# Keys and values projected between the two query chunks, the first attention two slots sooner

## The chip, the cores and the metric

The kernel runs on one core of one Trainium2 chip. The metric is the device time of one execution in microseconds (us), as the median of several runs; lower is better.

## The reference, cut to what matters

Two transformer-like blocks are computed for 256 tokens of width 1024. The first block projects the normed input into z, xbc, dt, q, k, v and gates, runs a state-space branch (a depthwise convolution of xbc, SiLU, a scan in two directions) and a window attention, mixes both with gates, and ends with an MLP. The second block has its own attention, a short convolution and an MLP. The change touches only the attention of the first block and the order in which its inputs are projected:

```python
proj = h @ w_in[l]
z, xbc, dt_raw, q, k, v, gates = split_cols(proj, IN_SPLITS)
...
logits = jnp.einsum('bnqgrd,bnkgd->bngrqk', qb, kb).astype(jnp.float32) * (ATTN_HEAD_DIM ** -0.5)
...
logits = jnp.where(valid[None, :, None, None], logits + bias, -jnp.inf)
m = jnp.maximum(jnp.max(logits, axis=-1, keepdims=True), sink_l)
p = jnp.exp(logits - m)
p = p / (jnp.sum(p, axis=-1, keepdims=True) + jnp.exp(sink_l - m))
out = jnp.einsum('bngrqk,bnkgd->bnqgrd', p.astype(v.dtype), vb)
```

There are 16 query heads and 4 key/value heads of 64. With 256 tokens there are two query blocks (token halves) of 128.

## The kernel before, in words

**Slots.** All weights are streamed from memory as 146 pieces of 1 MB plus the small dt piece, one for each of 147 slots, in an order written out by hand (`STRETCHES`, L119). SyncE issues the loads into a ring of three raw buffers. For each slot ScalarE rounds the piece into `w_hi` (`split_hi`, L1053) and VectorE computes the rest `w_lo` (`split_lo`, L1422), both two slots ahead of TensorE. TensorE multiplies three products (hi by hi, hi by lo, lo by hi) for each part (L393). The first slots are: 0 and 1 first half of the queries, 2 dt, 3 and 4 second half of the queries, 5 and 6 keys and values, 7 and 8 the first chunk of xbc, 9 and 10 of z, 11 to 24 seven more chunks of xbc.

**Work between the slots.** Every engine walks over the slots in the same program order, and side work is written into fixed places of this walk: the middle of a slot on TensorE (`slot_middle`, after half of its products) or its end. An engine takes its instructions in order, so a wait holds up all that is written behind it on that engine.

**The attention of the first block** is cut into eight units a = 0 to 7, each of four heads and one token half. Unit a goes through a pipeline of places:

- slot 7+a, end, TensorE: `scores` (L750), 8 small matmuls into banks 4 and 5.
- slot 7+a, VectorE: `softmax_sink` (L1564 to L1571), adds the bias table `bias1`, takes the maximum. Before it in the same slot stands `split_lo`.
- slot 8+a, ScalarE: `exps` (L1114); VectorE: `softmax_divide` (L1602, L1603), only the reciprocal, placed behind the `softmax_sink` of the next unit; GpSimd: `softmax_times` (L2059), multiplies the probabilities by it.
- slot 9+a, end, TensorE: `prob_turn` (L765), transposes half 0, then (after the scores of unit a+2) half 1 into bank 7; ScalarE: `prob_out` (L1149), copies both out.
- slot 10+a, middle, TensorE: `values1` (L775) into bank 7; ScalarE: `values_hi` (L1134); VectorE: `values_lo` (L1593), which frees bank 7.

The unit numbering takes all four query tiles of token half 0 first, then those of token half 1 (`r = a // 4`, `u = a % 4`).

**Other side work near it.** `softplus` and `minus_log_dt` (L1634 to L1651) compute dt and its negative logarithm on VectorE in small dependent steps; they stand in slots 4 and 6. `decay_sums` (L809) stands in slot 9. The convolution of chunk c: ScalarE copies it out (L1261) and applies the middle tap (L1268), VectorE applies the other four (`conv_taps`, L1663) in two halves of 8 instructions, chunk 0 in slots 9 and 10, chunk 1 in 13 and 14, chunk 2 in 15 and 16. SiLUs stand in slot 15 on ScalarE: the first chunk of z (L1238), then conv chunks 0 and 1 (L1144), which need another activation table than the exponentials; `exps` of unit 7 stands behind them in the same slot. `conv_turn` (L801) transposes finished chunks from slot 16 on.

The diff touches the places above in the programs of TensorE, ScalarE and VectorE, and the order of the pieces. GpSimd's and SyncE's programs keep their text.

Of the kernel before, what the change touches and what calls it, by code (L numbers as in the profile page):

```python
# [70 lines left out]

S_Q = 0
S_DT = 2
S_KV = 5
S_XBC = 7
S_Z0 = 9
S_XBC1 = 11
# [29 lines left out]
for _name, _width in PARAMS:  # L107
# [6 lines left out]
SILU_AT = {15: (0, 1), 19: (2, 3), 21: (4,), 23: (5,), 25: (6,)}  # L114
# [2 lines left out]


STRETCHES = [  # L119
    ("q", S_Q, "feat", 2), ("dt", S_DT, "dt", 1), ("q", S_DT + 1, "feat", 2), ("kv", S_KV, "kv", 2), ("xbc", S_XBC, "feat", 2),  # L120
    ("z", S_Z0, "tok", 2), ("xbc", S_XBC1, "feat", 14), ("z", S_Z, "tok", 6), ("gate", S_GATE, "tok", 8), ("ao", S_AO, "acc", 4), ("so", S_SO, "acc", 8),
    ("wo", S_WO, "acc", 4), ("mi", S_MI, "wide", 16), ("mo", S_MO, "acc", 16),
    ("q2", S_Q2, "tok", 2), ("k2", S_K2, "tok", 2), ("v2", S_V2, "tok", 2), ("cb2", S_CB2, "feat", 2),
# [1 line left out]
    ("ab2", S_AB2, "acc", 2), ("cv2", S_CV2, "acc", 2), ("wo2", S_WO2, "acc", 4),  # L125
    ("mi2", S_MI2, "wide", 16), ("mo2", S_MO2, "acc", 16),
]


def slot_table():  # L130
# [17 lines left out]
def build(nc, w_stream, w_dt, x_in, params_in, table_in, onehot_in, gate_bias_in, post_in, rpb_in,  # L148
# [3 lines left out]
    with ctx:  # L152
# [205 lines left out]
        def emptied(eng, key):  # L358

            eng.wait_ge(drained[where[key][0]], where[key][1] + 1)  # L360
# [12 lines left out]
        def _(pe):  # L373
# [367 lines left out]

            def scores(name, a, q_tile, k_tile):

                r = a // (4 if name == "a1" else 2)
                claim((name + "s", a, 0), 4)
                claim((name + "s", a, 1), 5)
                for h in range(2):
                    for e in range(2):
                        rows = slice(e * HD, e * HD + HD)
                        ins = pe.matmul(ps[:, 4 + e, h * TOK:h * TOK + TOK],  # L750
                                        q_tile(h)[rows, (1 - r) * P:(1 - r) * P + P], k_tile(h)[rows, :],
                                        start=True, stop=True)
                        if h:
                            ins.then_inc(*fill_of((name + "s", a, e)))
# [12 lines left out]
                ins.then_inc(*fill_of(key))  # L767

            def values1(a):
                kv = 2 * (a % 4 // 2)  # L770
                claim(("a1o", a), 7)
                emptied(pe, ("a1p", a, 1))
                for jt in range(RT):
                    for e in range(2):
                        ins = pe.matmul(ps[e * HD:e * HD + HD, 7, 0:2 * P],  # L775
                                        v_tok[:, jt, (kv + e) * HD:(kv + e) * HD + HD],
                                        prob_t1[a % 2][:, jt, 2 * e:2 * e + 2], start=jt == 0, stop=jt == 1)
                ins.then_inc(*fill_of(("a1o", a)))
# [95 lines left out]

            def slot_middle(s):

                if 0 <= s - 10 < 8:
                    values1(s - 10)
                if 0 <= s - 97 < 4:
                    values2(s - 97)  # L880
                if s in TURN_AT:
                    conv_turn(TURN_AT[s])
                if 0 <= s - 28 < GROUPS:
                    ssd_decay(s - 28, 1)
                if 0 <= s - 29 < GROUPS:
                    ssd_states(s - 29)
                    ssd_diagonal(s - 29)
                    ssd_across(s - 29)
# [8 lines left out]
            for s in range(SLOTS):  # L897
# [26 lines left out]
                if s == 0:  # L924
# [4 lines left out]
                    claim("rel", 4)  # L929
                    pe.matmul(ps[0:Q_HEADS, 4, :], table[:, :], onehot[:, :], start=True,  # L930
                              stop=True).then_inc(*fill_of("rel"))
                if s == 9:
                    decay_sums()

                if 0 <= s - 9 < 8:
                    prob_turn("a1", s - 9, 0, logit1)
                if s == S_DT + 1:

                    emptied(pe, "dt")
                    claim("dt_turn", 6)  # L940
                    for r in range(RT):
                        ins = pe.transpose(ps[:, 6, r * 64:r * 64 + 64], dt_feat[0:64, r * P:r * P + P],
                                           ident[0:64, 0:64])
                    ins.then_inc(*fill_of("dt_turn"))
                if 0 <= s - 7 < 8:
                    tile = 4 * ((s - 7) % 4 // 2) + 2 * ((s - 7) % 2)
                    if s == 7:
                        for c in range(2):
                            for h in range(2):
                                emptied(pe, ("q", c, h))  # L950
                        emptied(pe, ("kv", 0, 0)), emptied(pe, ("kv", 0, 1))
                    scores("a1", s - 7, lambda h: q_t[:, tile + h, :], lambda h: k_t[:, tile // 4, :])
                if 0 <= s - 9 < 8:
                    prob_turn("a1", s - 9, 1, logit1)
                if s == 17:
                    cumulate()

# [79 lines left out]
        def _(act):  # L1037
# [91 lines left out]
                                   ACT.Exp).then_inc(*drain_of(key))  # L1129

            def values_hi(a):
                r, tile = a // 4, 2 * (a % 4)
                ready(act, ("a1o", a))
                act.activation(ot_hi[:, tile:tile + 2, r * P:r * P + P],  # L1134
                               ps[:, 7, 0:2 * P].rearrange("p (h i) -> p h i", h=2),
                               ACT.Copy).then_inc(ot_hi_ready, 1)
# [50 lines left out]
            for s in range(SLOTS):  # L1187
# [35 lines left out]
                if s == S_DT + 1:  # L1223
                    act.wait_ge(dt_neg, 1)
                    act.activation(dtw[:, 2], dtw[:, 1], ACT.Exp).then_inc(dt_exp, 1)
                if 0 <= s - 10 < 8:
                    values_hi(s - 10)
                if s in TURN_AT:
                    c = TURN_AT[s]
                    ready(act, ("turn", c, 0))  # L1230
# [7 lines left out]
                    act.activation(zg(all_rows, 0, 512), zg(all_rows, 0, 512), ACT.Silu).then_inc(z_first_silu, 1)  # L1238
                for c in SILU_AT.get(s, ()):
                    conv_active(c)  # L1240
                if s == 9:
                    ready(act, "sums")
                    act.activation(sums[:, :, :], ps[:, 7, 0:4 * HEADS].rearrange("p (a b) -> p a b", a=4),
                                   ACT.Exp).then_inc(*drain_of("sums"))

                if 0 <= s - 8 < 8:
                    exps(s - 8, logit1, 0, True)

                if name == "xbc" and closes:
                    c = chunk  # L1250
# [13 lines left out]
                    for i in range(4):  # L1264
                        if i % 2 == 0:
# [1 line left out]
                        f = 4 * c + i  # L1267
                        act.activation(acc_of(c)[:, i, :], conv_in[k][:, i, PAD:PAD + TOK], ACT.Identity,  # L1268
                                       scale=conv_w[:, 2, f:f + 1], bias=conv_b[:, f:f + 1]).then_inc(conv_tap0, 1)
                if 0 <= s - 9 < 8:  # L1270
                    prob_out("a1", s - 9, 0, prob_t1)
                    prob_out("a1", s - 9, 1, prob_t1)
                if s == 18:
                    ready(act, "cum")
                    act.activation(cum_hi[:, :, :], ps[:, 6, :].rearrange("p (u l) -> p u l", u=4),
# [134 lines left out]
        def _(dve):  # L1410
# [139 lines left out]

            def softmax_sink(a):

                k, r, u = a % 2, a // 4, a % 4
                sink, at0 = param("sink"), P * (1 - r)
                if a == 0:
                    dve.wait_ge(bias1_landed, 16)
                if a >= 2:
                    ready(dve, ("a1p", a - 2, 1))
                for e in range(2):
                    key = ("a1s", a, e)  # L1560
                    ready(dve, key)
                    for h in range(2):
                        i, head = 2 * e + h, 8 * (u // 2) + 2 * (u % 2) + 4 * e + h
                        ins = dve.tensor_tensor_reduce(logit1[k][:, i, :], ps[:, 4 + e, h * TOK:h * TOK + TOK],  # L1564
                                                       bias1[:, head, at0:at0 + TOK], 1.0,
                                                       sink[:, 4 * u + i:4 * u + i + 1], ALU.add, ALU.max,
                                                       soft[:, k, 0, i:i + 1])
                    ins.then_inc(*drain_of(key))
                emptied(dve, ("a1s", a, 0)), emptied(dve, ("a1s", a, 1))
                link(dve.tensor_scalar(soft[:, k, 1, :], soft[:, k, 0, :], -1.0, None, ALU.mult))  # L1570
                dve.tensor_tensor(soft[:, k, 2, :], soft[:, k, 1, :], sink[:, 4 * u:4 * u + 4],  # L1571
                                  ALU.add).then_inc(negmax_ready, 1)
# [15 lines left out]
                dve.tensor_scalar(soft[:, k, 1, :], soft[:, k, 0, :], -1.0, None, ALU.mult).then_inc(negmax_ready, 1)  # L1588

            def values_lo(a):  # L1590
                r, tiles = a // 4, slice(2 * (a % 4), 2 * (a % 4) + 2)
                dve.wait_ge(ot_hi_ready, a + 1)
                dve.tensor_tensor(ot_lo[:, tiles, r * P:r * P + P],  # L1593
                                  ps[:, 7, 0:2 * P].rearrange("p (h i) -> p h i", h=2),
# [200 lines left out]
            for s in range(SLOTS):  # L1795
                if 0 <= s - 28 < GROUPS:
                    ssd_weigh(s - 28, 0)
                if 0 <= s - 10 < 8:
                    values_lo(s - 10)
                if s in TURN_AT:  # L1800
                    c = TURN_AT[s]
                    ready(dve, ("turn", c, 1))
# [25 lines left out]
                                             ALU.min).then_inc(dt_neg, 1)  # L1828
                if s == S_DT + 2:
                    softplus()  # L1830
                if s == S_DT + 4:
                    minus_log_dt()
                if 0 <= s - 7 < 8:
                    softmax_sink(s - 7)
                if 0 <= s - 8 < 8 and s not in SILU_AT:
                    softmax_divide(s - 8, logit1, 0, True)
                if s in TAPS_AT:
                    conv_taps(TAPS_AT[s], (0, 1))
                if s - 1 in TAPS_AT and s != LAST_TAPS:
                    conv_taps(TAPS_AT[s - 1], (2, 3))  # L1840
                if 0 <= s - 8 < 8 and s in SILU_AT:
                    softmax_divide(s - 8, logit1, 0, True)
                if s == 10:
                    emptied(dve, "sums")
                    for i in range(2):
# [278 lines left out]
def packed(inputs):  # L2124
# [17 lines left out]
    w2 = f["w_in_2"][0]  # L2142
    parts = []
    for stretch in (
        pieces_tok(q, 0, 2), pieces_tok(w_in, COL_KV, 1), pieces_tok(w_in, COL_XBC, 1),
        pieces_tok(w_in, COL_Z, 1), pieces_tok(w_in, COL_XBC + 512, 7), pieces_tok(w_in, COL_Z + 512, 3), pieces_tok(w_in, COL_GATE, 4), pieces_acc(ao),
        pieces_acc(f["w_ssd_out"][0]), pieces_acc(f["w_o"][0]), pieces_tok(f["w_mlp_in"][0], 0, 8),
        pieces_acc(f["w_mlp_out"][0]), pieces_tok(w2, 0, 10), pieces_acc(f["w_attn_branch_2"][0]),
# [68 lines left out]
```

## Time and profile before

| what | value |
|---|---|
| median of 3 runs | 947.56 us (947.48 to 947.64) |
| profiled execution, its own time | 949.15 us |
| its span, first to last instruction | 947.3 us |
| TensorE matmul busy | 935.9 us, 99% |
| VectorE busy | 666.1 us, 70% |
| ScalarE busy | 510.2 us, 54% |
| GpSimd busy | 78.8 us, 8% |
| mean granted TensorE clock | 0.998 |

The busy share of TensorE is modelled from pipelined matmuls, so it hides small gaps. The list of waits and the chain of work that ended last show where TensorE waited for another engine. Times in rows are microseconds from the start of the span.

### The profile page before, as it was taken

The numbers are of one execution on the slowest core, as the hardware profiler recorded it, in microseconds if no ns is written. First come the engines' busy times: TensorE is split into PE (matmuls) and PEld (weight loads), VectorE is DVE, ScalarE is ACT, GpSimd is POOL, SyncE is SP. The second block draws the span as 40 slices with busy tenths as digits, with TensorE's granted clock in tenths as the row PEclk, the third lists the DMA queues.
The fourth block names the chain that finished last, engine by engine and source line by source line (L and its number), as shares of the span: only waits on it lengthen the run. The fifth ranks groups of instructions, "written<-read, shape, count | busy, mean of one in ns | idle before, by whom it ended". The sixth has DMA issues, their size and how long they took to land.

```text
span 947.3 us, 13184 instructions
## 1 busy us (share of the span) xinstructions
PE 935.9 (99%) x5362; PEld 808.5 (85%) x5362; DVE 666.1 (70%) x917; ACT 510.2 (54%) x666; POOL 78.8 (8%) x76
## 2 busy tenths in 40 slices
PE   8999989999999999999999999999999999999998
PEld 7988879988888878888888888899888898888887
DVE  6779789998788764778776466767665758776433
ACT  6456886776545733465554335756653455554331
POOL 1002111023321000000002320000000000000000
PEclk9999999999999999999999999999999999999999
DMA  8943233555224385435556955353364435445551
GB/s 306 339 159 122 99 131 112 181 171 177 95 89 156 134 305 185 178 134 212 187 178 212 275 182 219 117 207 131 127 217 181 177 134 220 180 178 221 179 178 45
DMA packets 25276, 166.51 MB, mean 176 GB/s; under 512 B 2986, under 2 KB 3114, under 8 KB 6656
## 3 DMA queue, kind: packets, MB, share of 16 engines
q1 hardware_dynamic: 22464, 156.12, 46.0%
q0 software_dynamic: 2752, 9.54, 3.4%
q8 instruction: 43, 0.70, 0.3%
q14 instruction: 17, 0.14, 0.0%
HBM read 164.57 MB, written 1.08 MB: 175 GB/s over the span
## 4 chain that ended last, share of the span: by engine, by line
PE 90%; DVE 6%; ACT 2%; issue 1%; DMA 0%; DVEq 0%; ACTq 0%
PE ps L393 58%; PE ps L624 11%; PE ps L626 6%; DVE conv_acc L1663 2%; PE ps L821 1%; PE ps L750 1%; PE ps L765 1%; PE ps L424 1%; PE ps L426 1%; PE ps L433 1%; PE ps L512 1%; PE ps L590 1%; DVE logit L1564 1%; PE ps L871 1%; PE ps L801 1%
## 5 line engine op out<-in xcount | busy, mean ns | idle before, releaser
L1422 DVE TENSOR_TENSOR w_lo<-raw,w_hi 128x2048 fp32r<-128x2048 f32 x145 | 336.6, 2327 | 182.2 <-ACT w_hi L1053 182.1
L1053 ACT ACTIVATE w_hi<-raw 128x2048 fp32r<-128x2048 f32 x145 | 275.5, 1905 | 183.7 <-PE ps L393 161.9
L393 PE MATMUL ps<-w_hi,ht 128*128 128x512 f32 (+1 forms) x576 | 181.4, 388 | 0.0
L624 PE MATMUL ps<-ht,w_hi 128*128 128x512 f32 x448 | 158.4, 399 | 0.0
L393 PE MATMUL ps<-ht,w_hi 128*128 128x256 f32 (+1 forms) x816 | 151.3, 287 | 0.0
L393 PEld LDWEIGHTS ps<-ht,w_hi 128*128 128x128 f32 (+1 forms) x816 | 127.1, 192 | 3.3 <-issue 3.3
L393 PEld LDWEIGHTS ps<-w_hi,ht 128*128 128x128 f32 x576 | 107.3, 188 | 22.4 <-issue 1.1
L626 PE MATMUL ps<-ht,w_lo 128*128 128x256 f32 x448 | 125.8, 281 | 0.0
L393 PE MATMUL ps<-ht,w_lo 128*128 128x256 f32 (+1 forms) x408 | 115.7, 283 | 0.0
L393 PE MATMUL ps<-w_lo,ht 128*128 128x512 f32 (+1 forms) x288 | 110.5, 384 | 0.0
L624 PEld LDWEIGHTS ps<-ht,w_hi 128*128 128x128 f32 x448 | 84.2, 188 | 20.8
L393 PE MATMUL ps<-w_hi,ff_hi 128*128 128x512 f32 x256 | 99.7, 389 | 0.0
L393 PE MATMUL ps<-w_hi,ff_lo 128*128 128x512 f32 x256 | 99.6, 389 | 0.0
L393 PE MATMUL ps<-w_lo,ff_hi 128*128 128x512 f32 x256 | 99.6, 389 | 0.0
L626 PEld LDWEIGHTS ps<-ht,w_lo 128*128 128x128 f32 x448 | 84.6, 189 | 0.0
L393 PEld LDWEIGHTS ps<-ht,w_lo 128*128 128x128 f32 (+1 forms) x408 | 78.1, 191 | 0.0
L393 PEld LDWEIGHTS ps<-w_lo,ht 128*128 128x128 f32 x288 | 54.2, 188 | 10.5
L1663 DVE SCALAR_TENSOR_TENSOR conv_acc<-conv_in,params,conv_acc 128x256 f32<-128x256 f32 x128 | 58.9, 532 | 0.0
L393 PEld LDWEIGHTS ps<-w_hi,ff_hi 128*128 128x128 f32 x256 | 48.1, 188 | 10.1
L393 PEld LDWEIGHTS ps<-w_hi,ff_lo 128*128 128x128 f32 x256 | 48.0, 188 | 9.9
L393 PEld LDWEIGHTS ps<-w_lo,ff_hi 128*128 128x128 f32 x256 | 48.1, 188 | 9.9
L1161 ACT ACTIVATE ff_sum<-ps 128x512 f32<-128x512 f32 x32 | 18.8, 595 | 37.6 <-PE ps L626 32.6
(300 smaller groups left out, 1228.5 us busy)
## 6 DMA issues: line engine op xcount, KB each, us to landing
raw<-in_w_stream SPq DMA_DIRECT2D x145, 1024.0 KB, 4.8
bias<-rel_scratch POOLq DMA_DIRECT2D x1, 3072.0 KB, 21.4
bias<-in_rpb POOLq DMA_DIRECT2D x16, 128.0 KB, 8.3
x_first<-in_x_in SPq DMA_DIRECT2D x2, 512.0 KB, 4.1
raw<-in_w_stream SPq DMA_DIRECT2D x2, 512.0 KB, 6.3
gates<-in_gate_bias POOLq DMA_DIRECT2D x4, 256.0 KB, 5.9
gates<-in_gate_bias POOLq DMA_DIRECT2D x2, 512.0 KB, 7.7
x<-in_x_in POOLq DMA_DIRECT2D x1, 1024.0 KB, 8.4
```

Of the source, the lines that this page charges most:

```text
L393: ins = pe.matmul(o, still, moving, start=first and n == 0, stop=last and n == 2, skip_group_check=True)
L424: pe.matmul(ps[:, i, 0:TOK], hi[:, c], ht_hi[:, k, :], start=opens and kt == 0, stop=False, skip_group_check=True)
L426: pe.matmul(ps[:, i, 0:TOK], lo[:, c], ht_hi[:, k, :], start=False, stop=False, skip_group_check=True)
L433: ins = pe.matmul(ps[:, i, TOK:2 * TOK], hi[:, kt * 512 + i * P:kt * 512 + i * P + P], ht_lo[:, 4 * part + kt, :], start=False, stop=close ...
L512: pe.matmul(ps[:, bank0 + r, :], ht_hi[:, 4 * part + kt, tokens], w[:, kt * 512:kt * 512 + 512], start=part == 0 and kt == 0 and m == 0, s ...
L590: pe.matmul(ps[:, 2 * n + r, :], a_hi[:, kt, r * P:r * P + P], w[:, cols], start=kt == 0 and m == 0, stop=False, skip_group_check=True)
L624: pe.matmul(ps[:, b, :], hi[:, c], ht[:, :, k, :], start=opens and kt == 0, stop=False, skip_group_check=True)
L626: ins = pe.matmul(ps[:, b, 0:TOK], lo[:, c], ht_hi[:, k, :], start=False, stop=closes and kt == 3, skip_group_check=True)
L1053: act.activation(split_home(s)[0][:, 0:width(s)], raw[s % RAW_RING][:, 0:width(s)], ACT.Copy).then_inc(hi_ready, 1)
L1161: act.activation(ff_sum[half][:, :, :], ps[:, b:b + 2, TOK:2 * TOK], ACT.Copy).then_inc(lows_out, 1)
L1422: dve.tensor_tensor(lo[:, 0:width(s)], raw[s % RAW_RING][:, 0:width(s)], hi[:, 0:width(s)].bitcast(F32), ALU.subtract).then_inc(lo_ready, 1)
L1663: ins = dve.scalar_tensor_tensor(acc_of(c)[:, i, :], conv_in[k][:, i, tap:tap + TOK], conv_w[:, tap, f:f + 1], acc_of(c)[:, i, :], ALU.mul ...
```

## The change

The second query chunk and the keys and values swap places in the stream: slots 3 and 4 are keys and values, slots 5 and 6 the second query chunk. All places of the attention units move two slots ahead: scores in 5+a, exps and divide in 6+a, the turn in 7+a, values in 8+a. Units take another order: for query tiles 0 and 1 both token halves first (a = 0 to 3), then for tiles 2 and 3 (`unit1`). `decay_sums` with its ScalarE exponential moves from slot 9 to slot 6. `minus_log_dt` moves from slot 6 to slot 11, ahead of that slot's `softmax_sink`. The diff, cut where a line only repeats the shift:

```diff
@@ -71,7 +71,8 @@
 S_Q = 0
 S_DT = 2
-S_KV = 5
+S_KV = 3
+S_Q1 = 5
 S_XBC = 7
@@ -117,7 +118,7 @@
 STRETCHES = [
-    ("q", S_Q, "feat", 2), ("dt", S_DT, "dt", 1), ("q", S_DT + 1, "feat", 2), ("kv", S_KV, "kv", 2), ("xbc", S_XBC, "feat", 2),
+    ("q", S_Q, "feat", 2), ("dt", S_DT, "dt", 1), ("kv", S_KV, "kv", 2), ("q", S_Q1, "feat", 2), ("xbc", S_XBC, "feat", 2),
...
+def unit1(a):
+
+    return a // 2 % 2, 2 * (a // 4) + a % 2
...
             def scores(name, a, q_tile, k_tile):
 
-                r = a // (4 if name == "a1" else 2)
+                r = unit1(a)[0] if name == "a1" else a // 2
...
             def values1(a):
-                kv = 2 * (a % 4 // 2)
+                kv = 2 * (unit1(a)[1] // 2)
...
             def slot_middle(s):
 
-                if 0 <= s - 10 < 8:
-                    values1(s - 10)
+                if 0 <= s - 8 < 8:
+                    values1(s - 8)
...
-                if s == 9:
+                if s == 6:
                     decay_sums()
 
-                if 0 <= s - 9 < 8:
-                    prob_turn("a1", s - 9, 0, logit1)
+                if 0 <= s - 7 < 8:
+                    prob_turn("a1", s - 7, 0, logit1)
...
+                if 0 <= s - 5 < 8:
+                    tile = 2 * unit1(s - 5)[1]
+                    if s == 5:
+                        emptied(pe, ("kv", 0, 0)), emptied(pe, ("kv", 0, 1))
+                    if s in (5, 9):
+                        for h in range(2):
+                            emptied(pe, ("q", (s - 5) // 4, h))
+                    scores("a1", s - 5, lambda h: q_t[:, tile + h, :], lambda h: k_t[:, tile // 4, :])
                 if 0 <= s - 7 < 8:
-                    tile = 4 * ((s - 7) % 4 // 2) + 2 * ((s - 7) % 2)
-                    if s == 7:
-                        for c in range(2):
-                            for h in range(2):
-                                emptied(pe, ("q", c, h))
-                        emptied(pe, ("kv", 0, 0)), emptied(pe, ("kv", 0, 1))
-                    scores("a1", s - 7, lambda h: q_t[:, tile + h, :], lambda h: k_t[:, tile // 4, :])
-                if 0 <= s - 9 < 8:
-                    prob_turn("a1", s - 9, 1, logit1)
+                    prob_turn("a1", s - 7, 1, logit1)
@@ scalar
-                if 0 <= s - 10 < 8:
-                    values_hi(s - 10)
+                if 0 <= s - 8 < 8:
+                    values_hi(s - 8)
...
-                if s == 9:
+                if s == 6:
                     ready(act, "sums")
...
-                if 0 <= s - 8 < 8:
-                    exps(s - 8, logit1, 0, True)
+                if 0 <= s - 6 < 8:
+                    exps(s - 6, logit1, 0, True)
...
-                if 0 <= s - 9 < 8:
-                    prob_out("a1", s - 9, 0, prob_t1)
-                    prob_out("a1", s - 9, 1, prob_t1)
+                if 0 <= s - 7 < 8:
+                    prob_out("a1", s - 7, 0, prob_t1)
+                    prob_out("a1", s - 7, 1, prob_t1)
@@ vector
-                if 0 <= s - 10 < 8:
-                    values_lo(s - 10)
+                if 0 <= s - 8 < 8:
+                    values_lo(s - 8)
...
-                if s == S_DT + 4:
+                if s == 11:
                     minus_log_dt()
-                if 0 <= s - 7 < 8:
-                    softmax_sink(s - 7)
-                if 0 <= s - 8 < 8 and s not in SILU_AT:
-                    softmax_divide(s - 8, logit1, 0, True)
+                if 0 <= s - 5 < 8:
+                    softmax_sink(s - 5)
+                if 0 <= s - 6 < 8 and s not in SILU_AT:
+                    softmax_divide(s - 6, logit1, 0, True)
                 if s in TAPS_AT:
                     conv_taps(TAPS_AT[s], (0, 1))
...
@@ packed, the order of the pieces in memory
-        pieces_tok(q, 0, 2), pieces_tok(w_in, COL_KV, 1), pieces_tok(w_in, COL_XBC, 1),
+        pieces_tok(q, 0, 1), pieces_tok(w_in, COL_KV, 1), pieces_tok(q, 512, 1), pieces_tok(w_in, COL_XBC, 1),
```

## Rows read from the trace of the kernel before

**Rows 1.** The page: busy time of each engine (share of the span), instructions.

```profile
PE 935.9 (99%) x5362; PEld 808.5 (85%) x5362; DVE 666.1 (70%) x917; ACT 510.2 (54%) x666; POOL 78.8 (8%) x76
```

**Rows 2.** Waits of PE, 54 to 150 us: total, times, longest.

```profile
PE ps L775 <- ACT prob_t L1149: 1.8, 1, 1.8
PE ps L765 <- DVE ot_lo L1593: 1.3, 2, 1.0
```

**Rows 3.** Chain that ended last, 54 to 150 us: start, duration, what.

```profile
124.53 1.06 ACT conv_acc L1144
125.61 1.28 ACT L1114
...
131.27 1.74 PE ps L801 x8
133.00 3.73 PE ps L393 x24
...
137.61 2.88 PE ps L393 x24
...
141.53 1.02 PE ps L801 x8
```

**Rows 4.** PE in order of time: start, duration; in brackets the idle time before.

```profile
96.24 0.60 PE L765 MATMUL ps<-params,logit 128*128 128x128 f32 x4
...
124.89 0.66 PE L765 MATMUL ps<-params,logit 128*128 128x128 f32 x4 [0.97 <-DVE ot_lo L1593]
...
130.19 1.08 PE L775 MATMUL ps<-prob_t,v_tok 128*64 128x256 f32 x8 [1.77 <-ACT prob_t L1149]
```

**Rows 5.** Windows; the third number from the end is the granted clock.

```profile
131.00:131.50 0.50, 0.50 (x6) 0.30 (x3) 0.00 (x0) 0.50 (x1) 0.50 (x1) 0.92 0.33 131
...
131.50:134.50 3.00, 3.00 (x16) 3.00 (x15) 1.88 (x3) 1.70 (x4) 0.96 (x1) 0.50 0.01 3
135.00:138.50 3.50, 3.50 (x32) 3.50 (x31) 3.50 (x8) 1.73 (x4) 0.00 (x0) 1.00 0.41 115
```

**Rows 6.** DVE in order of time: first step of minus_log_dt, and what follows its last.

```profile
47.25 0.22 DVE L1638 TENSOR_SCALAR dtw<-dt 128x128 int32<-128x128 int32 x1
...
53.27 2.28 DVE L1422 TENSOR_TENSOR w_lo<-raw,w_hi 128x2048 fp32r<-128x2048 f32 x1
```

**Rows 7.** DVE in order of time, from the end of slot 9 to slot 15.

```profile
71.27 0.48 DVE L1564 CUSTOM_DVE_ANT_0 logit<-ps,bias,params 128x256 f32<-128x256 f32 x1 [2.07 <-PE ps L765]
...
73.66 4.86 DVE L1663 SCALAR_TENSOR_TENSOR conv_acc<-conv_in,params,conv_acc 128x256 f32<-128x256 f32 x8
...
88.67 2.27 DVE L1422 TENSOR_TENSOR w_lo<-raw,w_hi 128x2048 fp32r<-128x2048 f32 x1
90.87 0.47 DVE L1564 CUSTOM_DVE_ANT_0 logit<-ps,bias,params 128x256 f32<-128x256 f32 x1
...
93.14 0.18 DVE L1603 RECIPROCAL soft<-soft 128x4 f32<-128x4 f32 x1
...
126.95 3.25 DVE L1663 SCALAR_TENSOR_TENSOR conv_acc<-conv_in,params,conv_acc 128x256 f32<-128x256 f32 x8
```

**Rows 8.** POOL in order of time: the bias table's load, and one multiplication.

```profile
22.57 1.20 POOL L2035 DMA_DIRECT2D bias<-rel_scratch  x1 [4.56 <-DMA rel_scratch<-rel_row]
...
93.40 1.89 POOL L2059 TENSOR_TENSOR logit<-logit,soft 128x1024 f32<-128x1024 f32 x1 [7.85 <-DVE soft L1603]
```

**Rows 9.** The page's DMA issues: the bias table, us to landing.

```profile
bias<-rel_scratch POOLq DMA_DIRECT2D x1, 3072.0 KB, 21.4
```

**Rows 10.** Chain that ended last, 20 to 56 us: slots 4 to 7.

```profile
31.28 23.23 PE ps L393 x192
54.51 1.06 PE ps L750 x8
```

**Rows 11.** ACT in order of time: the table load of slot 19.

```profile
157.87 1.28 ACT L1144 ACT_TABLE_LOAD   x1
```

**Rows 12.** DVE in order of time, slot 18.

```profile
156.08 0.69 DVE L1726 TENSOR_TENSOR cum_lo<-ps,cum_hi 128x512 f32<-128x512 f32 x1 [1.93 <-ACT cum_hi L1275]
```

More of the change, by code:

```diff
@@ L1131, in values_hi @@
             def values_hi(a):
-                r, tile = a // 4, 2 * (a % 4)
+                r, u = unit1(a)
+                tile = 2 * u
                 ready(act, ("a1o", a))
@@ L1551, in softmax_sink @@
             def softmax_sink(a):
-                k, r, u = a % 2, a // 4, a % 4
+                k, (r, u) = a % 2, unit1(a)
                 sink, at0 = param("sink"), P * (1 - r)
@@ L1590, in values_lo @@
             def values_lo(a):
-                r, tiles = a // 4, slice(2 * (a % 4), 2 * (a % 4) + 2)
+                r, u = unit1(a)
+                tiles = slice(2 * u, 2 * u + 2)
                 dve.wait_ge(ot_hi_ready, a + 1)
@@ L1840, in _ @@
                     conv_taps(TAPS_AT[s - 1], (2, 3))
-                if 0 <= s - 8 < 8 and s in SILU_AT:
-                    softmax_divide(s - 8, logit1, 0, True)
+                if 0 <= s - 6 < 8 and s in SILU_AT:
+                    softmax_divide(s - 6, logit1, 0, True)
                 if s == 10:
```

## The prediction

> **What bounds the kernel now.** I read the page first: TensorE is busy 935.9 us, 99% of the span [rows 1]. The change adds and takes away no matmul, so it can only move waits of TensorE and its clock. The list of waits comes next. In the stretch that the change touches TensorE waits three times: twice for `values_lo` to free bank 7, 1.3 us together, once for `prob_out`, 1.8 us [rows 2]. TensorE in order of time gives each its place: 0.97 us before the second half-turn of slot 15 and 1.77 us before the values in the middle of slot 16 [rows 4]; the third is the rest, 1.3 - 0.97 = 0.3 us, at the end of slot 11. The chain explains the 1.77 us. In slot 15 ScalarE does the SiLUs, the last one ready only after VectorE's taps, then loads the table of the exponentials again for 1.28 us, and only then takes the exponentials of unit 7 and `prob_out` of unit 6, for which TensorE waits [rows 3].
>
> The windows show something behind it. The granted clock is 1.00 until 131, 0.50 from 131.4 to 134.5 at least, and 1.00 again from 135 [rows 5]: 2.4 GHz, 1.2 GHz, 2.4 GHz. Ahead of the fall stand the idle 0.97 and 1.77 us. The eight transposes of slot 16 take 1.74 us there against 1.02 in slot 17, and 24 matmuls 3.73 against 2.88 [rows 3]: (1.74 - 1.02) + (3.73 - 2.88) = 1.6 us. So this jam costs 0.97 + 1.77 + 1.6 = **4.3 us**.
>
> **What the change removes.** Exponentials end in slot 13 and the turns in slot 14, so no exponential stands behind slot 15's SiLUs; one 1.28 us load there and one in slot 19 go with it. Values of unit 7 stand in slot 15, before the SiLUs in ScalarE's order. At the end of slots 15 and 16 no half-turn waits for bank 7 any more. All of the 4.3 us goes. The 0.3 us at slot 11 stays, since taps of chunk 0 remain in slots 9 and 10 ahead of `values_lo`.
>
> **What it moves at no cost.** The matmuls of the stream are the same, 192 in 23.23 us for four slots [rows 10]. Swapping the pieces keeps sizes, count and ring order on SyncE and both splits. The copies of keys and values go to slots 3 and 4 on ScalarE, those of the second query chunk to 5 and 6; each takes the place of the other. The sums in slot 6 are the same instructions, under the exponential table as before. The eight units are the same work in another order. The first scores come after slot 5, at 31.28 + 2 x 5.81 = 42.9, done by 44.0. The bias table is issued at 22.57 and lands 21.4 us later, at 44.0 [rows 8, 9]; if its 1.2 us of issue come on top, 45.2. VectorE then waits 1.2 us, with only the split for slot 8 behind it (2.3 us, needed near 60), and TensorE does not wait. Cover gone would mean a landing after about 50, where the next scores want banks 4 and 5: bounded below by nothing, above by perhaps 1 us. I take 0. The table load removed in slot 19 is hidden: VectorE is synchronised with TensorE through ScalarE's copy in slot 18, for which it idles 1.93 us [rows 11, 12], so behind slot 18 all starts at the same distance from TensorE as before.
>
> **What it adds.** `minus_log_dt` leaves slot 6 for slot 11: 53.27 - 47.25 = **6.0 us** of dependent small steps [rows 6]. In slot 6 VectorE had room. In slot 11 the steps stand between the split for slot 13 and `softmax_sink` of unit 6, and behind that comes the reciprocal of unit 5. GpSimd multiplies only after it, and TensorE turns unit 5 at the end of slot 12. I follow this chain in the times of before, where units 4 and 3 stand in these places. All from the end of slot 9 is the same in both kernels: sink at 71.27, taps from 73.66, and so on with no idle time on VectorE, to the split of slot 11 at 88.67 and the sink at 90.87, the reciprocal at 93.14 [rows 7], GpSimd from 93.40 to 95.29 [rows 8]. TensorE comes to the turn at 96.24 to 96.4 [rows 4]. The slack is about 1 us. With 6.0 us put in ahead of the sink GpSimd ends at 101.3 and TensorE starts at 101.4: **a wait of 5.0 us**. Everything behind it on TensorE is late by that: scores of unit 7 and slot 13.
>
> Behind it I find no second wait. `prob_out` of unit 5 has ScalarE's exponentials of unit 6, a copy of chunk 1 and its four taps ahead of it, and ends near 106.0; its values are due at 106.4. The splits for slots 14 and 15 end near 103 and 111, due near 111 and 119. The taps of chunk 1 end near 116 and 122, SiLU of chunk 0 near 127, its turn is due near 129.
>
> **The clock.** No row shows TensorE idle for 5.0 us. The nearest is the 1.77 us stretch that was followed by the fall worth 1.6 us [rows 3 to 5]; the 0.97 us one alone was not. Lower bound 0, if the clock comes back before the wait ends; upper bound 3.2, two such stretches. I take 1.6, since this idle time is longer than one that did bring the clock down. The Trainium skill ("TensorE: Matmul & The Clock Gate", section "HAM oscillation — how this bites in real kernels") says that long idle gaps halve the clock, and prices the low time at one half of it; by that the 3.1 to 3.6 us seen at half speed would cost 1.6 to 1.8 us, and the sum would be up to 0.2 us higher. By that rule, too, the clock speaks against this change; the trace agrees as far as its one fall goes.
>
> **The sum.** 5.0 + 1.6 - 4.3 = **+2.3 us**. The profiled execution has 949.15 us, so 951.4 for it; it lies 1.6 us above the median of the runs, so 947.56 + 2.3 = **949.8 us**. A measurement of this kernel can tell about 0.2% from no change, that is 1.9 us: faster is below 945.7, slower above 949.5.
>
> **The rivals.**
> *A. Forecast:* the wait of 5.0 us in slot 12 with a fall of the clock. Between the bounds of the clock, some 0.9 to 3.2 us, it gives 949.1 to 951.5. Chance 0.60; about a quarter of it lies below 949.5.
> *B. The wait without the fall:* 5.0 - 4.3 = +0.7, 948.3 us, no measurable change. For it: the fall in before came after two waits close together, and the mean clock is 1.00 everywhere else. Against it: 5.0 us is nearly three times 1.77. Chance 0.17.
> *C. Faster:* VectorE gets to slot 11 early enough. The place is the taps of slots 9 and 10: they take 4.8 us each while GpSimd multiplies beside them, against 3.25 at 126.95 with GpSimd idle [rows 7]. If the new unit order and timing take that overlap away, the chain is 2 x 1.5 = 3.1 us shorter, the wait 1.9 us, and the time 947.56 - 4.3 + 1.9 = 945.2 us (946.8 with a fall). It decides from a wait under 2.4 us on. For it: nothing in the profile but the size of the effect. Against it: the reciprocal that starts GpSimd stands directly ahead of the taps in both kernels. The same chance holds the case that I misread the slack. Chance 0.13, with 943.3 us at the end where nothing waits.
> *D. A second wait behind the first:* `prob_out` of unit 5 is only 0.4 us ahead of its values. Should ScalarE's copy and taps of chunk 1 come 1.5 us later, TensorE waits again in the middle of slot 13: 951.3 us. Chance 0.10.
>
> **How the numbers follow.** The prediction is A's 949.8. Faster is C: 0.13. Same is B and a quarter of A: 0.17 + 0.15 = 0.32. Slower is the rest of A and D: 0.55. The range leaves out C and the ends of A and D: 947.4, a little under B, to 951.6, the upper bound of the clock's cost.
>
> **What the profile after should show.** TensorE's longest wait is some 5 us, at L765's turn in slot 12, put down to GpSimd's multiplication or to VectorE's reciprocal. On VectorE the steps of `minus_log_dt` stand in slot 11 right behind a split and end some 2.3 us before the reciprocal. The chain there runs over them instead of over TensorE. The waits for `prob_out` (1.77) and for `ot_lo` in slot 15 (0.97) are gone, and only one table load stands before slot 28's. The granted clock falls to 0.50 within a few us of the new wait and not near slot 16. Wrong would be: no wait over 2 us in slot 12 (C), a clock of 1.00 all through (B), or new waits in slots 5 to 8 for `bias1`.

## The result and the profile after

| | median us | runs | ratio to before, 95% interval |
|---|---|---|---|
| before | 947.56 | 947.35 to 949.05, 5 | |
| changed | 952.4 | 951.54 to 952.51, 5 | 1.0047 (1.0034 to 1.0060) |

The changed kernel is slower by 4.8 us in the medians, 0.5%. The forecast was +2.3 us, 949.8 (947.4 to 951.6): the direction was right, the time lies outside the range. The profiled execution of the changed kernel has 952.03 us, with a span of 950.2 us.

The list of waits of TensorE (PE) in the changed kernel, 54 to 160 us, total, times and longest, answers to [rows 2]:

```profile
PE ps L771 <- POOL logit L2067: 5.0, 1, 5.0
PE ps L771 <- DVE ot_lo L1601: 0.3, 1, 0.3
```

Both waits of the old jam, 1.77 and 0.97 us, are gone, the 0.3 us in slot 11 has stayed, and one wait of 5.0 us is new. L771 is the turn of a unit's probabilities (L765 before), L2067 GpSimd's multiplication. VectorE (DVE) in order of time in the changed kernel shows why GpSimd is late:

```profile
95.04 2.27 DVE L1429 TENSOR_TENSOR w_lo<-raw,w_hi 128x2048 fp32r<-128x2048 f32 x1
97.24 0.21 DVE L1646 TENSOR_SCALAR dtw<-dt 128x128 int32<-128x128 int32 x1
...
103.04 0.29 DVE L1659 SCALAR_TENSOR_TENSOR ndt<-dtw 128x128 f32<-128x128 f32 x1
103.25 0.48 DVE L1571 CUSTOM_DVE_ANT_0 logit<-ps,bias,params 128x256 f32<-128x256 f32 x1
...
105.53 0.18 DVE L1611 RECIPROCAL soft<-soft 128x4 f32<-128x4 f32 x1
```

The split for slot 13 ends, the 18 steps of `minus_log_dt` follow without a gap from 97.24 to 103.25, then the sink, then the reciprocal: [rows 7] with 6.0 us put in. The chain of work that ended last goes on from there:

```profile
105.78 1.90 POOL logit L2067
107.69 0.04 issue
107.73 1.11 PE ps L771 x4
108.84 2.01 PE ps L756 x8
110.85 1.04 PE ps L771 x4
111.90 3.46 PE ps L399 x24
115.36 1.01 PE ps L781 x8
```

Four transposes (L771) take 1.11 us here, the eight scores (L756) 2.01 and the second four transposes 1.04. The same three at full clock stand earlier in the same chain:

```profile
75.52 0.44 PE ps L771 x4
75.95 1.06 PE ps L756 x8
77.02 0.60 PE ps L771 x4
```

The 24 matmuls take 3.46, and took 2.88 in [rows 3]. The windows of the changed kernel show the granted clock, third number from the end, answering to [rows 5]:

```profile
102.70:105.70 3.00, 0.07 (x1) 0.00 (x0) 2.78 (x15) 0.25 (x1) 0.00 (x0) 1.00 0.01 3
106.00:106.50 0.50, 0.00 (x0) 0.00 (x0) 0.50 (x2) 0.50 (x4) 0.50 (x1) 0.78 0.00 0
106.50:107.70 1.20, 0.00 (x0) 0.00 (x0) 1.20 (x1) 1.20 (x7) 1.18 (x1) 0.50 0.00 0
107.70:113.00 5.30, 5.27 (x23) 4.12 (x24) 3.19 (x6) 4.40 (x9) 0.00 (x0) 0.50 0.38 124
113.50:117.00 3.50, 3.50 (x30) 2.84 (x28) 0.90 (x7) 1.42 (x3) 1.89 (x1) 1.00 0.10 40
```

The clock is 1.00 (2.4 GHz) until the wait is well under way, 0.50 (1.2 GHz) from about 106.3 on while TensorE is still idle (the mean of 0.78 puts the fall there), and 1.00 again from 113.5 at the latest. TensorE works some 5.3 us at half speed. That costs (1.11 - 0.44) + (2.01 - 1.06) + (1.04 - 0.60) + (3.46 - 2.88) = 2.6 us in this execution.

This alone would give 4.96 + 2.6 - 4.3 = +3.3 us between the two profiled executions; they differ by 952.03 - 949.15 = 2.9. But the medians differ by 4.8. The two comparisons disagree, and that is the first thing that the experiments had to clear up. There were two theories: theory one, the profiled execution of before is not like most of its runs; theory two, something else in slots 3 to 17 costs 2 us.

### The profile page after: what moved, and what is told of

Same layout as the page of the kernel before. It is cut to its first block, busy times and chain, and to the rows that moved or that the text cites. A ratio compares the mean times of both kernels' runs of the same rounds, so it can differ in the third digit from the quotient of the medians.

```text
span 950.2 us, 13182 instructions
## 1 busy us (share of the span) xinstructions
PE 937.4 (99%) x5362; PEld 809.3 (85%) x5362; DVE 666.6 (70%) x917; ACT 507.5 (53%) x664; POOL 78.7 (8%) x76
## 4 chain that ended last, share of the span: by engine, by line
PE 92%; DVE 5%; issue 1%; ACT 1%; POOL 0%; DVEq 0%; ACTq 0%
PE ps L399 59%; PE ps L630 11%; PE ps L632 6%; PE ps L827 1%; PE ps L756 1%; PE ps L771 1%; DVE conv_acc L1671 1%; PE ps L430 1%; PE ps L432 1%; PE ps L439 1%; PE ps L518 1%; PE ps L596 1%; PE ps L877 1%; PE ps L836 1%; PE ps L706 1%
```

## Experiments

**The kernel before once more**, unchanged, for the clock of each run.

> The kernel before, unchanged, to see the granted clock of each of its runs. My theory now: the fall of the clock behind the 1.77 us wait of slot 16 is in the profiled run (949.15 us, mean clock 0.998) but not in most runs, so most runs show a mean clock of 1.000 and about 947.5 us, and those with 0.998 about 949.1 us. Rival: the fall is in every run (0.998 each), and the 2 us by which the change was dearer than forecast come from somewhere in slots 3 to 17.

Measured: median 947.59, 11 runs. Nine lie between 947.42 and 947.77 with a mean clock of 1.000 or 0.999, two at 949.03 and 949.13 with 0.998. Of the 15 runs of before beside them, four lie at 949.06 to 949.14 with 0.998, the others at 947.38 to 947.71. The new profiled execution has a span of 945.8, mean clock 1.0, and the same waits of 1.8 and 1.3 us. Its windows, same columns:

```profile
128.50:130.00 1.50, 0.00 (x0) 0.00 (x0) 1.50 (x5) 1.50 (x7) 0.00 (x0) 1.00 0.79 311
131.00:131.50 0.50, 0.50 (x6) 0.27 (x3) 0.00 (x0) 0.50 (x1) 0.50 (x1) 1.00 0.48 197
131.50:134.50 3.00, 3.00 (x28) 3.00 (x27) 2.32 (x3) 1.62 (x4) 1.00 (x1) 1.00 0.01 3
```

The idle 1.5 us are there, and the clock stays at 1.00, with 28 matmuls in the 3.0 us where [rows 5] has 16. Its chain has the transposes and the matmuls of slot 16 at full speed:

```profile
130.22 1.08 PE ps L775 x8
131.31 1.02 PE ps L801 x8
132.33 2.88 PE ps L393 x24
```

So the 1.6 us of [rows 3] are no part of the usual execution: the profile I was given was one of the minority near 949.1 us. Theory one holds. Over all measurements of this kernel that minority is 15 of 64 runs.

**The logarithm left out.** It leaves out the logarithm of dt: one multiplication stands for the 18 steps.

```diff
             def minus_log_dt():
...
+                dve.tensor_scalar(ndt[:, :, :], dt[:, :, :], -1.0, None, ALU.mult).then_inc(ndt_ready, 1)
```

> The changed kernel with minus_log_dt cut from 18 small steps to one multiplication, in slot 11 as before. It leaves out the logarithm of dt. The wait of 4.96 us at the end of slot 12 goes, and with it the half-speed stretch that cost 2.65 us: 952.4 - 7.6 = 944.8 us, clock 1.000, no wait of TensorE over 0.5 us before 200 us. By the rival (2 us lost elsewhere in slots 3 to 17) it stays at 946.8 or above.

Measured: 944.58 us, 944.47 to 944.74, ratio 0.9964 (0.9952 to 0.9977), all five runs at a clock of 1.000. No wait of TensorE over 0.5 us is left before 200 us. From the usual execution of before, 947.57 - 944.58 = 3.0 us are gained, against 0.97 + 1.77 = 2.7 us of removed waits; no row explains the other 0.3 us. Nothing dearer is hidden in the early slots: theory two falls.

**The logarithm in three pieces**, complete, six steps each, ahead of the sinks of slots 6, 8 and 9 (the lines that divide the function are left out here).

```diff
...
-                if s == 11:
-                    minus_log_dt()
+                if s in (6, 8, 9):
+                    minus_log_dt((6, 8, 9).index(s))
```

> The changed kernel with minus_log_dt complete but cut into three pieces of about 2 us each, ahead of the softmax_sink of slots 6, 8 and 9, where VectorE idles 2.53, 2.10 and 2.03 us in the changed kernel's trace. If those idle times cover them: the same as without the logarithm, 944.8 us, within 0.3. If the smaller steps delay the sinks: each late sink delays GpSimd, which has 1 to 3 us of room there, so 945 to 947 us with a wait of TensorE at a turn in slots 7 to 10.

Measured: 944.63 us (944.54 to 946.23), ratio 0.9968 (0.9955 to 0.9980). It is as fast as without the logarithm. VectorE in order of time in this kernel:

```profile
48.66 0.22 DVE L1647 TENSOR_SCALAR dtw<-dt 128x128 int32<-128x128 int32 x1
...
49.95 0.95 DVE L1653 RECIPROCAL dtw<-dtw 128x128 f32<-128x128 f32 x1
52.13 0.48 DVE L1571 CUSTOM_DVE_ANT_0 logit<-ps,bias,params 128x256 f32<-128x256 f32 x1 [1.22 <-PE ps L756]
...
67.81 0.94 DVE L1660 SCALAR_TENSOR_TENSOR dtw<-dtw 128x128 f32<-128x128 f32 x3
69.19 0.48 DVE L1571 CUSTOM_DVE_ANT_0 logit<-ps,bias,params 128x256 f32<-128x256 f32 x1 [0.43 <-PE ps L771]
...
77.14 0.29 DVE L1662 SCALAR_TENSOR_TENSOR dtw<-dtw 128x128 f32<-128x128 f32 x1
77.47 0.29 DVE L1663 SCALAR_TENSOR_TENSOR ndt<-dtw 128x128 f32<-128x128 f32 x1
77.96 0.48 DVE L1571 CUSTOM_DVE_ANT_0 logit<-ps,bias,params 128x256 f32<-128x256 f32 x1 [0.20 <-PE ps L771]
```

Behind each piece VectorE still waits for TensorE, 1.22, 0.43 and 0.20 us: the pieces lie wholly in idle time. One of its five runs, 946.23 us, has a mean clock of 0.998, though no wait of the attention over 0.3 us is left in this kernel. This is the version that beats both kernels, by 2.9 us against before and 7.8 against the changed one.

**The logarithm behind the reciprocal.** One edit: in slot 11 `minus_log_dt` is called after `softmax_divide`, not ahead of `softmax_sink`.

> The changed kernel with minus_log_dt left whole in slot 11, but behind the softmax_divide of that slot instead of ahead of its softmax_sink. If the place ahead of the reciprocal is what costs, GpSimd is no longer late and the 4.96 us wait goes. The next thing behind the 6 us is values_lo of unit 4, which then frees bank 7 at about 106.1 where the second half-turn of slot 12 wants it at 104.2: a wait of 1.9 us. 944.8 + 1.9 = 946.7 us with the clock at 1.000, 948.3 us with a fall of it. If VectorE's load in that stretch is what costs, wherever the 6 us stand, it stays near 952.

Measured: 951.15 us, 949.61 to 952.52, ratio 1.0033 (1.0020 to 1.0046). GpSimd is no longer late, so the place ahead of the reciprocal made the 5.0 us. But the wait at bank 7 is 3.5 us, not 1.9. VectorE and GpSimd in order of time, and TensorE's turn:

```profile
99.80 0.20 DVE L1646 TENSOR_SCALAR dtw<-dt 128x128 int32<-128x128 int32 x1
100.03 1.91 DVE L1647 TENSOR_SCALAR dtw<-dt 128x128 int32<-128x128 int32 x1
101.98 0.23 DVE L1649 CAST dtw<-dtw 128x128 f32<-128x128 int32 x1
```

```profile
99.96 1.90 POOL L2067 TENSOR_TENSOR logit<-logit,soft 128x1024 f32<-128x1024 f32 x1 [7.85 <-DVE soft L1611]
```

```profile
107.96 1.11 PE L771 MATMUL ps<-params,logit 128*128 128x128 f32 x4 [3.50 <-DVE ot_lo L1601]
```

The second step takes 1.91 us instead of 0.23 and ends as GpSimd's multiplication ends: it was held for 1.7 us, the missing part of the wait. Without a fall of the clock the kernel would stand at 944.6 + 3.5 = 948.1; its runs lie 1.5, about 3.0 and 4.4 us above, with mean clocks of 0.998, 0.996 and 0.994. Only the first has a trace, with the clock at 0.50 from 108 to 111 us, right behind the wait; that the clock made all of the other two differences is inferred from their means.

**The move alone, in the kernel before.**

```diff
-                if s == S_DT + 4:
+                if s == 11:
                     minus_log_dt()
```

> The kernel before with one edit, minus_log_dt moved from slot 6 to slot 11. My theory: the whole loss of the change is this move, and the place of the pipeline doesn't matter to it. So a wait of 5.0 us for GpSimd at the end of slot 12, with a clock cost of 1.5 to 3 us behind it, on top of all that the kernel before has: 947.5 + 5.0 + 2.8 = 955.3 us. Rival: it costs that only with the attention two slots sooner, because then other work stands in slot 11; here under 950.

Measured: 954.84 us (954.68 to 955.41), ratio 1.0077 (1.0064 to 1.0089). Its waits, same columns as above:

```profile
PE ps L765 <- POOL logit L2059: 5.0, 1, 5.0
PE ps L775 <- ACT prob_t L1149: 1.8, 1, 1.8
PE ps L765 <- DVE ot_lo L1593: 1.3, 2, 1.0
```

The same 5.0 us wait and 7.3 us in all, on top of the old jam; 2.3 us of them are more than the wait. The move cost the changed kernel 7.8 us in the first measurement and 6.9 in the second (952.4 and 951.5 against 944.6). So the loss is the move's, in either place of the pipeline. In this execution the clock is 0.50 from 99.5 to 106, and 1.00 behind the old jam's 1.77 us.

**The changed kernel with the logarithm back in slot 6**, the same edit the other way.

> The changed kernel with minus_log_dt whole and back in slot 6. There it stands between the split that ends at 49.1 and the sink of unit 1. The sink is then done at 57.4 instead of 53.9, GpSimd's multiplication of unit 0 at 59.6, and the turn of unit 0 is due at 57.5: a wait of about 2.2 us in slot 7, so 944.6 + 2.2 = 946.8 us, 948.3 where the clock falls once. If slot 6 had the room that it had in the kernel before: 944.6.

Measured: 951.08 us, 949.50 to 951.81, ratio 1.0033 (1.0020 to 1.0045). A wait in slot 7 came, but of 3.8 us, not 2.2. VectorE and GpSimd:

```profile
57.34 0.18 DVE L1611 RECIPROCAL soft<-soft 128x4 f32<-128x4 f32 x1
57.44 2.26 DVE L1429 TENSOR_TENSOR w_lo<-raw,w_hi 128x2048 fp32r<-128x2048 f32 x1
```

```profile
57.61 3.84 POOL L2067 TENSOR_TENSOR logit<-logit,soft 128x1024 f32<-128x1024 f32 x1 [33.51 <-DVE soft L1611]
```

Now the split started first, by 0.17 us, and GpSimd's multiplication takes 3.84 us instead of 1.89; it ends 1.75 us after the split does. TensorE's turn waits for it:

```profile
61.50 0.65 PE L771 MATMUL ps<-params,logit 128*128 128x128 f32 x4 [3.76 <-POOL logit L2067]
```

Without a fall the kernel would stand at 944.6 + 3.8 = 948.4; its runs lie 1.1 to 3.4 us above, with mean clocks of 0.998 and 0.996. Slot 6 no longer had the room that it had in the kernel before, since the sink of unit 1 stands there now. Slots 8 and 9, where VectorE idles 2.1 and 2.0 us, were not tried with the whole logarithm of 6.0 us.

**The jam of before by itself**: in slot 15 the exponentials of unit 7 stand ahead of the SiLUs on ScalarE, in the kernel before.

```diff
                 if s == 15:
+                    exps(7, logit1, 0, True)
...
-                if 0 <= s - 8 < 8:
+                if 0 <= s - 8 < 7:
                     exps(s - 8, logit1, 0, True)
```

> The kernel before with one edit on ScalarE: in slot 15 the exponentials of unit 7 stand ahead of the SiLUs instead of behind them. The 1.77 us wait of slot 16 goes, the 0.97 us one of slot 15 stays: 947.5 - 1.8 = 945.8 us. The clock should no longer fall in a part of the runs, so no run near 947.3. If the gain of the change's first part is not this wait: 947.5.

Measured: 945.75 us median, 11 runs, ratio 0.9982 (0.9973 to 0.9991). Ten runs at 945.58 to 945.89, one at 947.19 with a clock of 0.998. The 1.77 us are gone as expected. One run still has the lower mean clock, so the statement that no run would was too strong.

**The old unit order** in the three-piece version: `unit1` returns `(a // 4, a % 4)`, and TensorE checks the second query chunk at slot 7.

> The three-piece version (944.63 us) with the old order of units, all four query tiles of token half 0 first, and TensorE's check of the second query chunk at slot 7 instead of 9. The copies of that chunk end at 50.5, slot 7 ends near 58, so nothing waits: 944.6 us, the unit order being worth nothing. If the order matters, the scores of unit 2 wait for the chunk and it is slower by what they wait.

Measured: 944.70 us, 8 runs, ratio 0.9970 (0.9960 to 0.9981), two of them at 946.1 with a clock of 0.998. The order of units is worth nothing here.

**The changed kernel once more**, for its clock.

> The changed kernel, unchanged, to see the spread of its clock cost. Without any fall it would stand at 944.6 + 4.96 = 949.6 us. If each half-speed stretch costs about 1.5 us, as the kernel before and the displaced variants suggest (947.5 and 949.1; 949.6, 951.1 and 952.5), the runs lie near 951.1 and 952.6 with the wait of 5.0 us in each, and none at 949.6.

Measured: 951.51 us, 951.20 to 952.23, ratio 1.0035 (1.0022 to 1.0049). Three runs near 951.4, two near 952.1, none at 949.6: every run pays for the clock, 1.6 to 2.6 us here, 1.9 to 2.9 in the five runs of the first measurement. The two medians, 952.4 and 951.51, would then differ in how many runs have a longer stretch at half speed; both profiled executions, at 952.03 and 952.06, are of the longer kind, so no trace shows the shorter one.

**Half of the logarithm moved away**: ten steps in slot 6, eight left in slot 11.

> The changed kernel with the first ten of the 18 steps of minus_log_dt in slot 6 and the other eight, 2.6 us, left in slot 11. The steps in slot 6 fit (2.5 us idle and 1 us of room of GpSimd). The wait at the end of slot 12 shrinks by the 3.4 us that left slot 11, from 5.0 to 1.6 us: 944.6 + 1.6 = 946.2 us without a fall of the clock, 947.7 with one. A wait as long as the 1.77 us of the kernel before: if the length of the wait decides on the clock, a part of the runs falls, as there.

Measured: 946.47 us, 11 runs, ratio 0.9989 (0.9980 to 0.9997). The wait is 1.4 us, the bulk of the runs at 946.23 to 946.55. Two have 947.7 with a clock of 0.998. Two more, 948.13 and 948.77 at a clock of 1.000, I can't explain. The profiled execution is one of the 0.998 ones, and the fall is not behind this wait. Its windows far behind the attention:

```profile
405.00:409.50 4.50, 3.05 (x21) 2.24 (x20) 2.70 (x8) 2.14 (x7) 0.00 (x0) 1.00 0.00 0
409.50:410.00 0.50, 0.50 (x6) 0.50 (x5) 0.50 (x3) 0.50 (x2) 0.00 (x0) 0.70 0.00 0
410.00:413.00 3.00, 3.00 (x16) 3.00 (x16) 2.56 (x5) 1.62 (x1) 0.00 (x0) 0.50 0.00 0
```

It stands at the start of the MLP, where TensorE is busy 3.05 of 4.5 us before it and waits 1.24 us for the residual. So a run of any of these kernels at 1.5 us above its group need not owe it to the attention. The two versions with the logarithm in three pieces say the same: without the jam, 3 of their 13 runs still have 0.998, as large a share as the 15 of 64 of before. The 0.998 runs of before other than the profiled one have no trace with the place, and where their fall lies stays open.

## Why the prediction missed

**What bounds the kernel, what is removed.** Right in the waits: 0.97 and 1.77 us went, 0.3 stayed. Wrong in the step "this jam costs 0.97 + 1.77 + 1.6 = 4.3 us". The 1.6 us of half speed were in the profiled execution, but the usual run has none of them: only 15 of 64 runs of before have the longer time at all, and whether theirs lies at the jam is open. The sign stood in the table: 949.15 us for the profiled execution beside 947.48 to 947.64 for the runs. I read that gap of 1.6 us as an offset of profiling and carried it unchanged into the forecast; it was the very term that I then counted as a gain. The usual jam costs 2.7 us by its waits, 3.0 us as measured. Rival C's end, 943.3 us where nothing waits, was too low for the same reason: measured 944.6.

**What moves at no cost.** Right. `log_out` and `log_pieces` stand at 944.6, where the removed waits put them. The sink of unit 0 waited 0.70 us for the bias table, less than the 1.2 us allowed, and TensorE not at all. VectorE in order of time in the changed kernel, this sink and the first taps:

```profile
44.80 0.48 DVE L1571 CUSTOM_DVE_ANT_0 logit<-ps,bias,params 128x256 f32<-128x256 f32 x1 [0.70 <-DMA bias<-rel_scratch]
...
80.03 4.87 DVE L1671 SCALAR_TENSOR_TENSOR conv_acc<-conv_in,params,conv_acc 128x256 f32<-128x256 f32 x8
```

**The added wait.** Right to 0.1 us: forecast 5.0, measured 4.96, in the place and for the engine named. The same wait came in the kernel before with that one line moved.

**No second wait behind it.** Right; rival D did not come. Nor did C: the taps of slots 9 and 10 took 4.8 us again, the first of them in the row above.

**The clock.** The fall was foreseen, its size was not: 1.6 taken, 2.6 us in the profiled execution, 1.6 to 2.9 over ten runs, inside the bounds of 0 and 3.2. TensorE worked 5.3 us at half speed here against some 3.3 in [rows 5]. The lower bound of 0 rested on the clock coming back before the wait ends; it fell inside the wait instead. The Trainium skill ("TensorE: Matmul & The Clock Gate", section "HAM oscillation — how this bites in real kernels") prices low time at one half of it. The trace agrees for the low time in which TensorE works, half of 5.3 being 2.65; half of the whole low stretch of some 6.8 us would be too much, since 1.4 us of it passed in the wait.

**The sum by its steps.** Forecast 5.0 + 1.6 - 4.3 = +2.3. With what was measured, 5.0 + 2.8 (952.4 - 944.6 - 5.0) - 3.0 = +4.8. Of the 2.5 us missed, 1.3 lie in the jam and 1.2 in the clock. By its terms, the step that failed most is the 1.6 us counted into the jam's gain, and next to it the size of the clock's cost. The range was too narrow because both ends were built on a gain of 4.3 us: I put bounds on the clock's cost of the new wait, but none on that of the old one, though it was the same kind of event. With a gain of 2.7 us and all else as it was, the forecast would have been 951.5 us and the upper end 953.1, and 952.4 would have lain inside.

## What to carry to other kernels

When the profiled execution is slower than the shown runs by more than their spread, look for what only it has, and compare like with like: the stretch at half clock behind the 1.77 us wait was in one execution of this kernel and not in another. Before a chain of small steps is moved on an in-order engine, follow what stands behind it to the engine that waits last; 6 us ahead of one reciprocal cost 5.0 us of waiting on TensorE and the clock's share behind it, and cut into pieces of 2 us in front of waits that are there anyway they cost nothing. Two edits that arrive together should be timed apart: here the one gained 3.0 us and the other lost 7.8.

## What the runs showed of the hardware

The price of a wait on TensorE comes with a part that varies from run to run. With attention waits of 1.77 us or less most runs kept the full clock (by their times 49 of 64 of the kernel before and 10 of 13 of the two versions in three pieces, which have no such wait over 0.3 us). With 3.5 to 5.0 us all 25 runs have a mean clock of 0.998 or less and lie 1.1 to 4.4 us above the time that the wait alone gives. In the changed kernel's trace the clock fell to 0.50 some 3.5 us into the wait; with the logarithm back in slot 6 it fell about 1 us after the wait of 3.8 us had ended.

VectorE and GpSimd held each other up, both ways. GpSimd's multiplication first: a VectorE step of 0.23 us took 1.91. VectorE's split first: the multiplication of 1.89 us took 3.84. In the changed kernel's own trace the split that starts at 105.93, 0.15 us after the multiplication, takes 3.89 us instead of 2.27. The Trainium skill ("SBUF — State Buffer", section "🔬 SBUF: two separate sides") calls the pair of ports that the two share an exclusive lock, held for the whole instruction by the one that starts first; it says so for VectorE operations with two SBUF inputs or in a mode that uses two ports. The split has two SBUF inputs, and its traces agree. The step of 0.23 us has one, and no view names its mode; it was held all the same. The lock also fits the 4.8 us of the taps beside GpSimd against 3.25 without it [rows 7], but no run here took the multiplication away from them.
